# Routing tile by tile inside the mixer, with overflow work moved onto GpSimd, in a two-layer hybrid decoder trunk

## The chip, the cores and the metric

One core of one Trainium2 chip runs the whole program in one launch. The metric is device time in microseconds (us). The engines are TensorE (PE, with its weight loads as PEld), VectorE (DVE), ScalarE (ACT), GpSimd (POOL) and SyncE (SP), which mostly issues DMAs.

## The reference, cut to what matters

There are 1024 tokens of width 1024 and two layers. Layer 0 mixes tokens with an mLSTM and a gated linear attention side by side, layer 1 with sliding-window attention. Behind each mixer stands a mixture of experts: 4 groups of 8 experts, of which a token takes the best group and in it the best two experts.

```python
def hierarchical_moe(u, wg, bg, we, be, w_gate, w_up, w_down):
...
    g_probs = jax.nn.softmax((xt @ wg).astype(F32) + bg.astype(F32), axis=-1)
    g_p, g_idx = lax.top_k(g_probs, 1)
    e_logits = ((xt @ we).astype(F32) + be.astype(F32)).reshape(t, N_GROUPS, EXPERTS_PER_GROUP)
    e_in_group = jnp.take_along_axis(e_logits, g_idx[:, :, None], axis=1)[:, 0]
    top_l, top_i = lax.top_k(e_in_group, TOP_K)
    gates = g_p * jax.nn.softmax(top_l, axis=-1)
...
    padded = (counts + MOE_BLOCK - 1) // MOE_BLOCK * MOE_BLOCK
...
        return (jax.nn.silu(xb @ w_gate[e]) * (xb @ w_up[e])) @ w_down[e]
...
    out = jnp.zeros((t, d), F32).at[tok_buf].add(y_buf.astype(F32) * w_buf[:, None])
...
    for layer in range(DEPTH):
        j = layer // 2
        u = rmsnorm(h, mix_norm[layer])
...
        h = h + mix.astype(h.dtype)
        u = rmsnorm(h, ffn_norm[layer])
        h = h + hierarchical_moe(u, router_group_w[layer], router_group_b[layer], router_expert_w[layer],
...
    return rmsnorm(h, final_norm)
```

## The kernel before

The residual rows h stay in SBUF, 8 tiles of 128 tokens. A layer is a chain of blocks, and all engines meet between two of them: `layer0` or `layer1` (mixer and router product), `route` (choice of experts and the tables of rows), `experts` (one block of up to 128 rows for each of 32 experts), `experts_over` (blocks beyond the first of an expert, at run time), and last `finish`.

**layer0** (L135 to L1225) works on eight tiles in a software pipeline over t = 0 to 10. Tile t has its scores, states and heads; tile t-2 = u has `turn_out` (L537, transposes of the mixed rows) and `project_out` (L551, the output product), tile t-3 = v has `turn_rows` (L564, transposes for the router), `route_product` (L577), `turn_logits` (L585). The order on TensorE is written out in `between` (L589): pieces of the output product fill the gaps between the pieces of the newest tile. On GpSimd `gate_outputs` (L340, L343) multiplies the mixed rows by their gates, which lie in four slots that are loaded again. On VectorE the residual is added in halves (`residual`, L1164), `router_rows` (L1170, L1177) makes the normed rows, which are stored to DRAM (`u_rows`) and turned for the router; `take_logits` (L1180) adds the bias; `probabilities` (L1099) and `mask_att` (L1106) follow the scores of the newest tile. ScalarE has `h_root` (L875, squares and root), `router_cols` (L881) and `copy_logits` (L887).

**layer1** (L1866 to L2480) has the same tail: `project_out` (L2126, products on L2022), `residual` (L2413), `router_rows` (L2418), `turn_rows` (L2132), `route_product` (L2140), `turn_logits` (L2151).

**route** (L1228 to L1431) works for all eight tiles at once: some 30 VectorE instructions choose two experts a token, four wide matmuls rank the tokens of each expert (L1280 to L1283), some 40 VectorE instructions find places and columns, 32 matmuls make the tables of rows (L1287), four instructions finish them (L1425 to L1431). SP loads the first six expert units (1 MB each) in this block (`first_units`, L1852, L1858).

**experts** (L1439 to L1730). An expert has six units of 1 MB (gate, up and down, two halves each). ScalarE rounds a unit (`make_hi`, L1630), VectorE subtracts for the remainder (`make_lo`, L1691), TensorE multiplies three times (L1579). Rows come with an indirect DMA that GpSimd issues (`gather`, L1529) and go back with another (`scatter`, L1516). `turn_x` (L1563, L1566) transposes the gathered rows, `x_high` and `x_low` (L1695) split them, `silu_times_up` (L1702) and `hid_low` (L1706) stand between the products. GpSimd runs in a fixed order for expert e: scatter of e-1, gather of e+3, then `finish`, which waits until the scatter has landed. Both have this form, with two pairs of buffers:

```python
nc.gpsimd.tensor_copy(idx_y[j][:], rows_y[:, ds(e, 1)])   # L1519; gather L1530
pool.drain()                                              # L1520; gather L1531
pool.indirect_dma_start(...)                              # L1521; gather L1532
```

Of the kernel before, what the change touches and what calls it, by code (L numbers as in the profile page):

```python
# [73 lines left out]

def make_constants(nc, mem, A):

    c = {}
    for name, shape, dt in (
# [4 lines left out]
        ("by_channel", [P, 44], F32), ("channel_rows", [44, P], F32),  # L83
# [5 lines left out]
              ("conv_b", A["ab_conv_b"][0], 4)] + [(f"conv_w{j}", A["ab_conv_w"][0, j], 4) for j in range(CONV_K)]  # L89
    at, row_loads = 0, []  # L90
# [19 lines left out]
def fill_patterns(nc, c, pool):  # L110
# [20 lines left out]
    nc.gpsimd.memset(c["tri_gla"][0:GLA_CHUNK, GLA_CHUNK:P], 0.0)  # L131
    pool.drain()


def layer0(nc, c, A, h, row_loads, const_loads, logits, router, gate_rows, u_rows):  # L135
# [5 lines left out]
    T, SLOTS, RAW, UNITS = 8, 4, 3, 9  # L141
    with ExitStack() as ctx:
        mem = Memory(nc, ctx, "l0")
        with ExitStack() as under:
            u_hi, u_lo = split_tensor(Memory(nc, under, "l0u"), "u", [P, T, 8, P])
# [12 lines left out]
        slots = mem.sb("slots", [P, SLOTS, 1024])  # L158
        s_odd = [mem.sb(f"s_odd{j}", [P, 2, DV]) for j in range(2)]
# [5 lines left out]
        with ExitStack() as under:  # L165
            first = Memory(nc, under, "l0s")
            small_raw = first.sb("small_raw", [P, 8, 40])
            small_hi, small_lo = split_tensor(first, "small", [P, 8, 40])
        shifted = mem.sb("shifted", [P, T, 4, P])
        arena = mem.sb("arena", [P, 4 * (CONV_K - 1 + 1024) + 4096])  # L170
# [19 lines left out]
        root, scale, logit_cols, square = mem.sb("root", [P, T]), mem.sb("scale", [P, T]), mem.sb("logit_cols", [36, P]), mem.sb("square", [P, DV])  # L190
# [5 lines left out]
        P_, Q_ = bank(2), bank(3)  # L196
        inter_of = lambda t: pairs[1 if t == 0 else 0][:, 0:720].rearrange("p (h n) -> p h n", h=4)
# [11 lines left out]
                 "logits_copied", "logits_turned", "logits_made")  # L209
# [14 lines left out]
        with nc.Block() as block:  # L224

            @block.sync
            def _(sp):
# [28 lines left out]
                sp.dma_start(router[:, :, 0:4], A["router_group_w"][0].rearrange("(p k) n -> p k n", p=P)).then_inc(s["router_ready"], 16)  # L256
                sp.dma_start(router[:, :, 4:36], A["router_expert_w"][0].rearrange("(p k) n -> p k n", p=P)).then_inc(s["router_ready"], 16)
# [23 lines left out]
                load_gates(3)  # L281
                load_x_again(0)
                load_x_again(1)
                for t in range(T):
# [4 lines left out]
                    if t + SLOTS < T:  # L289
                        sp.wait_ge(stored[t % SLOTS], 16 * (t // SLOTS + 1))  # L290
                        sp.wait_ge(s["r_turned"], 2 * t + 2)
                        load_gates(t + SLOTS)
                for j in range(SLOTS):
                    sp.wait_ge(stored[j], 16 * 2)
# [3 lines left out]
            def _(pool):  # L298
# [41 lines left out]
                def gate_outputs(t):  # L340
                    pool.wait_ge(s["rows_scaled"], t + 1)
                    pool.wait_ge(gates_ready[t % SLOTS], 16 * (t // SLOTS + 1))
                    g.tensor_tensor(h[:, t], h[:, t], slots[:, t % SLOTS], ALU.mult).then_inc(s["rows_gated"], 1)  # L343

# [3 lines left out]
                for t in range(T):  # L348
                    gate_outputs(t)
                    if t + 3 < T:  # L350
                        end_keys(t + 3)

            @block.tensor
            def _(pe):
# [182 lines left out]
                def turn_out(u, half):  # L537
                    if half == 0:
# [4 lines left out]
                        if u >= 2:  # L543
                            pe.wait_ge(s["logits_made"], u - 1)
# [19 lines left out]
                def turn_rows(u, half):  # L564
                    if half == 0:
                        pe.wait_ge(s["r_rows_made"], u + 1)
                        if u + 1 < T:
                            pe.wait_ge(s["o_lo_made"], 2 * u + 4)
                        else:
                            pe.wait_ge(s["logits_made"], u)  # L570
                    else:
                        pe.wait_ge(s["r_cols_made"], 2 * u + 1)
                    for k in range(4 * half, 4 * half + 4):
                        last = nc.tensor.transpose(Q_[:, (k % 4) * P:(k % 4 + 1) * P], slots[:, u % SLOTS, k * P:(k + 1) * P], c["ident"][:])
                    last.then_inc(s["r_turned"], 1)

                def route_product(u):  # L577
                    pe.wait_ge(s["r_cols_made"], 2 * u + 2)
                    if u == 0:
                        pe.wait_ge(s["router_ready"], 32)  # L580
                    for k in range(8):
                        last = mm(Q_[0:36, 0:P], router[:, k], r_cols[:, k], start=(k == 0), stop=(k == 7))
                    last.then_inc(s["r_done"], 1)

                def turn_logits(u):  # L585
                    pe.wait_ge(s["logits_copied"], u + 1)
                    nc.tensor.transpose(Q_[:, 0:36], logit_cols[:], c["ident"][0:36, 0:36]).then_inc(s["logits_turned"], 1)

                def between(t, part):  # L589
# [6 lines left out]
                    elif part == 0:  # L596
                        if late:
                            project_out(u - 1, 1, 5, 7)
                    elif part == 1:
# [7 lines left out]
                    elif part == 3:  # L607
                        if here:
                            project_out(u, 0, 0, 4)
                    elif part == 4:  # L610
                        if here:
                            project_out(u, 0, 4, 8)
                        if late:
                            turn_rows(u - 1, 0)
                    elif part == 5:
                        if here:
                            project_out(u, 1, 0, 2)
                        if late:
                            turn_rows(u - 1, 1)
                    elif part == 6:  # L620
                        if here:
                            project_out(u, 1, 2, 4)
                        if late:
                            route_product(u - 1)
# [604 lines left out]

# [204 lines left out]

# [1132 lines left out]
```

## Time and profile before

| | us |
|---|---|
| median of 3 runs (lowest, highest) | 2441.41 (2437.42, 2445.01) |
| profiled execution, its own time | 2433.56 |
| its span | 2431.8 |
| PE, DVE, ACT, POOL busy | 2121.2, 1553.9, 1335.4, 419.3 |
| mean granted TensorE clock | 0.929 of full speed |

In the span the stages lie so: layer0 0 to 585, route 586.5 to 622.2, experts 622.9 to about 1248, layer1 1254 to 1716.6, route 1717.7 to 1753, experts 1753.9 to about 2383, finish to the end. No overflow block runs: in `experts_over` GpSimd clears one tile and the block ends. A timeline line gives the start, the length, the engine, the line, output and input, and in brackets the idle time of the engine just before and what ended it.

### The profile page before, as it was taken

How to read it: one execution, taken by the hardware profiler on the slowest of the kernel's cores; microseconds unless marked ns; L12 is line 12 of the kernel's file. 1: busy time of each engine (PE TensorE's matmuls, PEld its weight loads, DVE VectorE, ACT ScalarE, POOL GpSimd, SP SyncE). 2: the span in 40 equal slices, each digit the busy share in tenths (PEclk: the TensorE clock that was granted, in tenths of full speed). 3: DMA queues.
4: the chain of work that ended last, by engine and by line, in shares of the span. 5: the costliest groups of instructions: out<-in, count | busy, mean ns of one | idle time of the engine just before them, and what ended most of it. 6: DMA issues, size and time to landing. Idle time of an engine off the chain costs nothing. (4 is left out here: it accounts for less than half of the span.)

```text
span 2431.8 us, 29766 instructions
## 1 busy us (share of the span) xinstructions
PE 2121.2 (87%) x10467; PEld 1735.8 (71%) x10467; DVE 1553.9 (64%) x1591; ACT 1335.4 (55%) x1648; POOL 419.3 (17%) x381
## 2 busy tenths in 40 slices
PE   6989998985699999999959988899389999999990
PEld 5768876774588777877747867778378777777780
DVE  3551234443688888887845367623488888888885
ACT  4322334541488777777743256622078777777772
POOL 1200001110123222222213400000012222222220
PEclk9989998997799999999979978999699999999995
DMA  3112212113499999999943020000289999999975
GB/s 120 35 44 78 77 53 105 53 61 121 175 371 382 371 361 348 360 362 343 369 177 111 1 78 1 1 27 35 116 313 374 356 354 357 369 360 352 359 280 224
DMA packets 122120, 512.90 MB, mean 211 GB/s; under 512 B 27133, under 2 KB 28218, under 8 KB 87226
## 3 DMA queue, kind: packets, MB, share of 16 engines
q1 hardware_dynamic: 102458, 474.08, 52.7%
q0 software_dynamic: 18432, 33.60, 3.7%
q10 hardware_dynamic: 1152, 4.19, 0.5%
q8 instruction: 47, 0.77, 0.1%
q14 instruction: 31, 0.25, 0.0%
HBM read 495.02 MB, written 50.33 MB: 224 GB/s over the span
## 5 line engine op out<-in xcount | busy, mean ns | idle before, releaser
L1691 DVE TENSOR_TENSOR exp_w_lo<-ring_raw,exp_w_hi 128x2048 fp32r<-128x2048 f32 x384 | 866.4, 2289 | 105.5 <-ACT exp_w_hi L1630 104.9
L1630 ACT ACTIVATE exp_w_hi<-ring_raw 128x2048 fp32r<-128x2048 f32 x384 | 729.0, 1917 | 154.9 <-PE exp_y_out L1579 78.0
L1579 PE MATMUL exp_gate_out<-exp_w_hi,exp_x_hi 128*128 128x512 f32 x512 | 208.2, 407 | 11.8 <-DVE exp_w_lo L1691 10.7
L1579 PE MATMUL exp_y_out<-exp_w_hi,exp_hid_hi 128*128 128x512 f32 x512 | 211.7, 413 | 3.8 <-DVE exp_hid_lo L1706 3.8
L1579 PE MATMUL exp_y_out<-exp_w_lo,exp_hid_hi 128*128 128x512 f32 x512 | 205.4, 401 | 0.0
L1579 PE MATMUL exp_y_out<-exp_w_hi,exp_hid_lo 128*128 128x512 f32 x512 | 204.7, 400 | 0.0
L1579 PE MATMUL exp_gate_out<-exp_w_hi,exp_x_lo 128*128 128x512 f32 x512 | 201.9, 394 | 0.0
L1579 PE MATMUL exp_gate_out<-exp_w_lo,exp_x_hi 128*128 128x512 f32 x512 | 201.7, 394 | 0.0
L1579 PE MATMUL exp_up_out<-exp_w_hi,exp_x_lo 128*128 128x512 f32 x512 | 199.3, 389 | 0.0
L1579 PE MATMUL exp_up_out<-exp_w_hi,exp_x_hi 128*128 128x512 f32 x512 | 199.2, 389 | 0.0
L1579 PE MATMUL exp_up_out<-exp_w_lo,exp_x_hi 128*128 128x512 f32 x512 | 199.2, 389 | 0.0
L1521 POOL DMA_INDIRECT y_rows<-exp_y,exp_idx_y x64 | 114.1, 1783 | 374.1 <-issue 374.1
L1532 POOL DMA_INDIRECT exp_x_rows<-u_rows,exp_idx_u x64 | 101.3, 1583 | 423.4 <-DMA y_rows<-exp_y,exp_idx_y 370.0
L2022 PE MATMUL l_wide<-l_w_hi,l1s_work 128*128 128x512 f32 x512 | 170.6, 407 | 4.0 <-DVE l_w_lo L2349 3.5
L1695 DVE TENSOR_TENSOR exp_x_lo<-exp_x_turned,exp_x_hi 128x1024 fp32r<-128x1024 f32 x64 | 78.3, 1224 | 104.1 <-ACT exp_x_hi L1634 104.1
L1566 PE MATMUL exp_x_turned<-base_ident,exp_x_rows 128*128 128x128 f32 x512 | 75.5, 296 | 62.2 <-DMA exp_x_rows<-u_rows,exp_idx_u 61.9
L1634 ACT ACTIVATE exp_x_hi<-exp_x_turned 128x1024 fp32r<-128x1024 f32 x64 | 64.7, 1011 | 116.6 <-PE exp_x_turned L1566 116.6
L1579 PEld LDWEIGHTS exp_gate_out<-exp_w_hi,exp_x_hi 128*128 128x128 f32 x512 | 97.5, 190 | 31.6 <-issue 13.0
L1566 PEld LDWEIGHTS exp_x_turned<-base_ident,exp_x_rows 128*128 128x128 f32 x512 | 63.9, 151 | 76.6 <-DMA exp_x_rows<-u_rows,exp_idx_u 71.5
L1579 PEld LDWEIGHTS exp_y_out<-exp_w_hi,exp_hid_hi 128*128 128x128 f32 x512 | 100.9, 197 | 23.6 <-DVE exp_hid_lo L1706 4.3
L2022 PEld LDWEIGHTS l_wide<-l_w_hi,l1s_work 128*128 128x128 f32 x512 | 97.9, 191 | 27.6 <-DVE l_w_lo L2349 3.7
L1579 PEld LDWEIGHTS exp_y_out<-exp_w_hi,exp_hid_lo 128*128 128x128 f32 x512 | 99.6, 194 | 21.8
(418 smaller groups left out, 4016.1 us busy)
## 6 DMA issues: line engine op xcount, KB each, us to landing
ring_raw<-in_expert_w_gate_dram SPq DMA_DIRECT2D x128, 1024.0 KB
ring_raw<-in_expert_w_up_dram SPq DMA_DIRECT2D x128, 1024.0 KB, 11.7
ring_raw<-in_expert_w_down_dram SPq DMA_DIRECT2D x128, 1024.0 KB, 8.3
l0w_raw<-in_ab_w_in_dram SPq DMA_DIRECT2D x48, 256.0 KB, 2.8
l_q<-y_rows SPq DMA_DIRECT2D x8, 1024.0 KB, 5.1
finish_y<-y_rows SPq DMA_DIRECT2D x8, 1024.0 KB
base_h<-in_x_dram ACTq DMA_DIRECT2D x8, 512.0 KB, 6.9
gate_rows<-l0w_stage SPq DMA_DIRECT2D x16, 256.0 KB, 2.0
```

The costliest lines, as they stand in the source:

```text
L1521: pool.indirect_dma_start(y_rows, bass.IndirectOffsetOnAxis(ap=idx_y[j][:], axis=0), y[j][:], None, bounds_check=2047, oob_is_err=False).t ...
L1532: pool.indirect_dma_start(x_rows[j][:], None, u_rows, bass.IndirectOffsetOnAxis(ap=idx_u[j][:], axis=0), bounds_check=1023, oob_is_err=Fal ...
L1566: last = nc.tensor.transpose(x_turned[:, k], x_rows[j][:, k * P:(k + 1) * P], c["ident"][:])
L1579: last = nc.tensor.matmul(out, x[:, k0 + k], w[:, k, cols], start=(first and k == 0 and t == 0), stop=(last_unit and k == K - 1 and t == 2))
L1630: nc.scalar.activation(split[split_slot(unit)][0][:], raw[raw_slot(unit)][:], ACT.Copy).then_inc(hi_ready, 1)
L1634: nc.scalar.activation(x_hi[:], x_turned[:], ACT.Copy).then_inc(x_hi_s, 1)
L1691: nc.vector.tensor_tensor(lo[:], raw[raw_slot(unit)][:], hi[:].bitcast(F32), ALU.subtract).then_inc(lo_ready[split_slot(unit)], 1)
L1695: nc.vector.tensor_tensor(x_lo[:], x_turned[:], x_hi[:].bitcast(F32), ALU.subtract).then_inc(x_cols_s, 1)
L2022: last = nc.tensor.matmul(out_cols[:, cols], x[:, k], w[:, k, cols], start=(k == 0 and n == 0), stop=(k == 7 and n == 2))
```

## The change

1. `route` is gone. After a tile's logits VectorE chooses its experts (`choose_experts`, 16 instructions of a [128, 4] or [128, 32] size, most with a drain behind), TensorE ranks its tokens (`rank`, two matmuls) and enters them in the table (`enter`, two matmuls), one and two tiles late, in part 5 of `between`. The last tile's share and `make_tables` end layer0 and layer1.
2. The router reads rows of h that are not normed: the ffn gains are multiplied into the router on GpSimd once, the transposes take h itself, the scale is put in with the bias. The product has the rows stationary and the 36 router columns moving, so `copy_logits` and `turn_logits` go. `router_rows` becomes `scale_of` and `normed_rows`; the latter is called later in VectorE's order and only the store waits for it.
3. The gates' multiplication goes from GpSimd to VectorE (`gate_rows_of`), with three slots for four; the clearing of the two gather tiles too.
4. What is needed for overflow blocks alone (number of blocks, first columns, columns of tokens, one-hot marks, owners) is 76 GpSimd instructions in six pieces among the first six scatter and gather pairs of `experts`. Sixteen matmuls and a second `make_tables` for it end `experts`.
5. The first six expert units are loaded in layer0 and layer1; `experts` begins with `make_hi` of two units, and the weights of the two choices are worked out in it.
6. In layer 1 output product, residual and row transposes go by halves, and the order by tiles is changed with them.

```diff
-                gather(0, 0)
-                gather(1, 1)
-                for e in (2, 3):
-                    pool.wait_ge(x_turned_s, e - 1)
-                    gather(e, e % 2)
...
+                for e in range(4):
+                    if e < 2:
+                        pool.wait_ge(zeroed, e + 1)
+                    else:
+                        pool.wait_ge(x_turned_s, e - 1)
+                    gather(e, e % 2)
+                def scatter_and_gather(pair, q):
+                    e = 2 * pair + 1 + q
+                    scatter(e - 1, q)
+                    pool.wait_ge(x_turned_s, e + 2)
+                    gather(e + 3, q)
+                    finish(q, pair)
+                scatter_and_gather(0, 0)
+                count_blocks()
+                scatter_and_gather(0, 1)
+                first_columns()
+                scatter_and_gather(1, 0)
+                columns_of_tokens()
+                scatter_and_gather(1, 1)
+                mark_rest(0, 8)
+                scatter_and_gather(2, 0)
+                mark_rest(8, N)
+                scatter_and_gather(2, 1)
+                owners()
+                with pool.Fori(3, last_pair - 1) as pair:
...
+                def first_columns():
+                    g.tensor_copy(extra[:], above[:, 0:E, 0])
+                    g.tensor_copy(nth[:], above[:, E:, 0])
+                    pool.drain()
...
+                    for step in (1, 2, 4, 8, 16):
+                        g.tensor_copy(b[:, 0:step], a[:, 0:step])
+                        g.tensor_tensor(b[:, step:], a[:, step:], a[:, 0:E - step], ALU.add)
+                        pool.drain()
+                        a, b = b, a
...
+                def mark_rest(first_n, end_n):
+                    for n in range(first_n, end_n):
+                        g.tensor_scalar(slot_hot[:, n], c["iota"][:], slot[:, n:n + 1], None, ALU.is_equal)
+                        last = g.tensor_scalar(block_hot[:, n], c["iota"][:, 0:N_OVER], column[:, n:n + 1], value[:, n:n + 1], ALU.is_equal, ALU.mult)
...
+def choose_experts(v, dve, c, R, logits, t):
...
+    v.tensor_tensor(R.masked, R.masked, logits[:, t, 4:36], ALU.add)
+    for k in range(2):
+        dve.drain()
+        v.tensor_reduce(R.top[:, k, t:t + 1], R.masked, AX.X, ALU.max)
+        dve.drain()
+        v.scalar_tensor_tensor(R.flags, R.masked, R.top[:, k, t:t + 1], far, ALU.is_ge, ALU.mult)
...
                     elif part == 5:
                         if here:
                             project_out(u, 1, 0, 2)
                         if late:
-                            turn_rows(u - 1, 1)
+                            route_product(u - 1)
+                        if 1 <= u - 1 < T - 1:
+                            rank(u - 2, ranks)
+                        if 2 <= u - 1 < T - 1:
+                            enter(u - 3, entered)
+                        if t == T + 2:
+                            enter(T - 2, last_entered)
+                            rank(T - 1, last_ranks)
+                            enter(T - 1, last_entered)
+                            count()
```

## Rows read from the trace of the kernel before

**Rows 1.** The page: busy time by engine; ScalarE's costliest group, with its mean in ns.
```profile
PE 2121.2 (87%) x10467; PEld 1735.8 (71%) x10467; DVE 1553.9 (64%) x1591; ACT 1335.4 (55%) x1648; POOL 419.3 (17%) x381
...
L1630 ACT ACTIVATE exp_w_hi<-ring_raw 128x2048 fp32r<-128x2048 f32 x384 | 729.0, 1917 | 154.9 <-PE exp_y_out L1579 78.0
```

**Rows 2.** Busy time by stretch: window, length, PE, PEld, DVE, ACT, POOL, clock, DMA share, GB/s.
```profile
400.00:450.00 50.00, 49.62 (x334) 39.27 (x333) 23.23 (x53) 23.96 (x73) 6.17 (x6) 1.00 0.19 64
572.17:637.88 65.71, 17.97 (x74) 15.09 (x74) 29.18 (x95) 9.92 (x13) 6.14 (x8) 0.53 0.29 112
1702.28:1768.80 66.52, 21.92 (x117) 18.98 (x116) 30.21 (x98) 11.18 (x17) 6.03 (x8) 0.60 0.28 110
```

**Rows 3.** Timeline of PE between the mixers' last output products and the experts' first products.
```profile
571.77 0.39 PE L560 MATMUL l_pair<-l_w_hi,l_o_lo 128*128 128x512 f32 x1
580.41 3.63 PE L582 MATMUL l_pair<-l_r_cols,base_router 128*36 128x128 f32 x16 [0.69 <-ACT l_r_cols L885]
...
637.88 0.77 PE L1579 MATMUL exp_gate_out<-exp_w_hi,exp_x_hi 128*128 128x512 f32 x1 [5.33 <-DVE exp_w_lo L1691]
...
1702.04 0.39 PE L2022 MATMUL l_wide<-l_w_hi,l1s_work 128*128 128x512 f32 x1
```

**Rows 4.** Timeline of POOL at the start of both expert stages, and of DVE in route.
```profile
622.91 1.84 POOL L1512 MEMSET exp_x_rows<- 128x1024 f32 x2 [84.87 <-POOLq L57]
...
1753.93 1.84 POOL L1512 MEMSET exp_x_rows<- 128x1024 f32 x2 [341.22 <-POOLq L57]
...
590.25 0.22 DVE L1299 SCALAR_TENSOR_TENSOR route_flags<-base_iota,route_flags 128x64 f32<-128x64 f32 x1
590.55 0.22 DVE L1301 TENSOR_REDUCE route_idx<-route_flags 128x8 f32<-128x64 f32 x1
```

**Rows 5.** Timeline of layer 0's mixer: DVE, then POOL's gate product.
```profile
426.59 0.69 DVE L1104 SCALAR_TENSOR_TENSOR l_prob<-l_pair,l_shifted 128x512 f32<-128x512 f32 x1 [7.03 <-PE l_pair L466]
...
437.67 2.14 DVE L1177 SCALAR_TENSOR_TENSOR l_slots<-base_h,l_scale,l_gain_row 128x1024 f32<-128x1024 f32 x1
...
535.69 2.35 POOL L343 TENSOR_TENSOR base_h<-base_h,l_slots 128x1024 f32<-128x1024 f32 x1 [21.99 <-ACT base_h L866]
```

**Rows 6.** Layer 0's first expert stage: busy times, and what its PE waited for.
```profile
640.00:1230.00 590.00, 567.14 (x2624) 468.20 (x2624) 498.07 (x282) 444.98 (x313) 148.62 (x118) 0.98 0.95 357
PE exp_x_turned L1566 <- DMA exp_x_rows<-u_rows,exp_idx_u: 20.7, 10, 3.3
```

**Rows 7.** Lines L1531 and L1532: duration min/median/max in ns; time to landing.
```profile
L1531 POOLq DRAIN  x64: 242/9109/10644, 624.9 to 2325.9; - x64
DMA to landing us min/median/max: 4.1/8.6/10.7
```

**Rows 8.** Timeline of POOL in the first experts of layer 0.
```profile
677.16 1.68 POOL L1530 COPY exp_idx_u<-moe_rows_u 128x1 int32 x1
684.48 2.34 POOL L1532 DMA_INDIRECT exp_x_rows<-u_rows,exp_idx_u  x1 [5.63 <-DMA y_rows<-exp_y,exp_idx_y]
...
734.88 1.95 POOL L1530 COPY exp_idx_u<-moe_rows_u 128x1 int32 x1
742.47 2.23 POOL L1532 DMA_INDIRECT exp_x_rows<-u_rows,exp_idx_u  x1 [5.64 <-DMA y_rows<-exp_y,exp_idx_y]
...
764.61 0.20 POOL L1519 COPY exp_idx_y<-moe_rows_y 128x1 int32 x1
773.00 2.33 POOL L1521 DMA_INDIRECT y_rows<-exp_y,exp_idx_y  x1 [8.19 <-issue]
```

**Rows 9.** Timeline in the same stretch: PE's transposes of gathered rows, DVE's subtractions.
```profile
701.88 1.03 PE L1566 MATMUL exp_x_turned<-base_ident,exp_x_rows 128*128 128x128 f32 x8
...
734.49 4.53 DVE L1691 TENSOR_TENSOR exp_w_lo<-ring_raw,exp_w_hi 128x2048 fp32r<-128x2048 f32 x2 [0.52 <-ACT exp_w_hi L1630]
```

**Rows 10.** Groups of POOL instructions, shapes apart: count, busy us, mean ns, idle before.
```profile
L1519 POOL COPY exp_idx_y<-moe_rows_y 128x1 int32 x56 | 48.9, 873 | 57.1 <-ACT exp_y L1650 57.1
L1530 POOL COPY exp_idx_u<-moe_rows_u 128x1 int32 x56 | 41.1, 734 | 0.0
```

More of the change, by code:

```diff
@@ new lines, in rank_tokens, with take_ranks, mark_places @@
+def rank_tokens(mm, c, R, logits, t, ranks):
+    mm(ranks, c["tri_strict"][:], R.both[:, t], start=True, stop=False)
+    return mm(ranks, c["ones"][:], logits[:, t, 4:36], start=False, stop=True)
+def take_ranks(v, R, t, ranks):
+    return v.tensor_tensor(R.work, R.hot[:, :, t], bc(ranks, 1, 2), ALU.mult)
+def mark_places(v, dve, c, R, t):
+    v.tensor_reduce(R.pos[:, :, t], R.work, AX.X, ALU.add)
+    v.tensor_tensor(R.block_hot[t % 2], R.hot[:, :, t], bc(c["value"][:, :, t], 2, N_EXPERTS), ALU.mult)
+    dve.drain()
+    for k in range(2):
+        last = v.tensor_scalar(R.slot_hot[t % 2][:, k], c["iota"][:], R.pos[:, k, t:t + 1], None, ALU.is_equal)
+    return last
@@ new lines, in enter_tokens, with take_entries, make_tables @@
+def enter_tokens(mm, R, t, entered):
+    for k in range(2):
+        last = mm(entered, R.slot_hot[t % 2][:, k], R.block_hot[t % 2][:, k], start=(k == 0), stop=(k == 1))
+    return last
+def take_entries(v, R, t, entered):
+    if t == 0:
+        return v.tensor_copy(R.made[:], entered)
+    return v.tensor_tensor(R.made[:], R.made[:], entered, ALU.add)
+def make_tables(v, dve, made, rows_y, rows_u, none, table):
+    v.tensor_scalar(none, made, 0.0, float(UNUSED + 1), ALU.is_equal, ALU.mult)
+    dve.drain()
+    v.scalar_tensor_tensor(table, made, -1.0, none, ALU.add, ALU.add)
+    dve.drain()
+    v.tensor_copy(rows_y[:], table)
+    dve.drain()
+    return v.tensor_scalar(rows_u[:], rows_y[:], 1, None, ALU.logical_shift_right)
@@ new lines, in load_first_units, with moe @@
+def load_first_units(sp, A, layer, raw, raw_ready):
+    for m, (name, e) in enumerate((("expert_w_gate", 0), ("expert_w_up", 0), ("expert_w_gate", 1))):
+        src = A[name][layer, e].rearrange("(p a k) n -> a p k n", p=P, a=2)
+        for half in range(2):
+            s = 2 * m + half
+            sp.dma_start(raw[s][:].rearrange("p (k n) -> p k n", k=4), src[half]).then_inc(raw_ready[s], 16)
+def moe(nc, c, A, layer, R, logits, weight, u_rows, y_rows, raw, raw_ready):
+    with ExitStack() as ctx:
+        Memory(nc, ctx, f"ring{layer}").sb("raw", [P, len(raw), 2048])
+        experts(nc, c, A, layer, R, logits, weight, u_rows, y_rows, raw, raw_ready)
+    experts_over(nc, c, A, layer, R, u_rows, y_rows)
@@ L89, in make_constants @@
               ("conv_b", A["ab_conv_b"][0], 4)] + [(f"conv_w{j}", A["ab_conv_w"][0, j], 4) for j in range(CONV_K)]
+    params += [(f"ffn_gain{layer}", A["ffn_norm"][layer], 8) for layer in range(2)]
     at, row_loads = 0, []
@@ L609, in between @@
                             project_out(u, 0, 0, 4)
+                        if late:
+                            turn_rows(u - 1, 1)
                     elif part == 4:
@@ L1866, in layer1 @@
-def layer1(nc, c, A, h, weight, y_rows, logits, router, u_rows):
+                    if 0 <= w < T - 1:
+                        normed_rows(w)
+                take_late_entries(T - 2)
+                place_late(T - 1)
+                take_late_entries(T - 1)
+                make_tables(v, dve, R.made[:], R.rows_y, R.rows_u, R.masked, R.flags)
+                dve.wait_ge(s["counted"], 1)
+                v.tensor_copy(R.counts[:], counted)
+def layer1(nc, c, A, h, weight, y_rows, logits, router, u_rows, R, raw_ring, ring_ready):
```

1383 lines of the change are left out of this document (715 added, 668 removed).

## The prediction

> **What bounds the kernel now.** I read the page first. PE is busy 87% of the span, POOL 17% [rows 1]; that average hides three regimes, so I asked for busy times by stretch. In the steady mixer of layer 0 PE is busy 49.62 of 50 us: work added to PE there is added time. Between the last output product of a mixer and the first expert product PE has 18.0 of 65.7 us and 21.9 of 66.5 us of work [rows 2]; that is where the change can win. In the expert stage of layer 0 PE is busy 567 of 590 us, and all but 2 us of the rest is its wait for gathered rows, ten times, 20.7 us in all [rows 6]. So GpSimd, nearly idle in the page, runs a chain whose pace is that of PE or a little worse: index copy, drain, indirect DMA, twice an expert. The reader should see what the chain is made of: the copy is a column of 128 numbers, but the drain behind it has a median of 9.1 us, against 0.24 us when nothing is in flight, about a landing (8.6 us) [rows 7]. In the timeline the gather at 684.48 stands 5.6 us behind the copy begun at 677.16, and the scatter at 773.00 stands 8.2 us behind its copy [rows 8]. What is added to this chain behind a landing moves the next gather one for one, and PE with it once the lead is used up. The lead: gather of expert 4 is issued at 684.48, lands 8.6 later at 693, and is needed at 701.88 [rows 8, 9], so 8 to 9 us; expert 7's is issued at 742.47, landed by 751, and needed three PE periods of 17.71 after 701.88, at 755.0: 4 us are left.
>
> **What is saved, layer 0.** The last product ends at 572.16 and the expert stage begins at 622.91 [rows 3, 4]: 50.7 us. What takes its place: 3.4 us from that end to the router product (8.2 now, at 580.41 [rows 3]; the normed rows, 2.1 us [rows 5], leave the path, and so do the transposes and copies of the first half, done earlier; between 3 and 5); the product at the cold clock 3.6 [rows 3], 16 matmuls as now; the logits 0.5; `choose_experts`, 16 dependent instructions at the 0.30 us between two such in route [rows 4], 4.8; six matmuls of rank and enter at 0.23 each (3.63 by 16 [rows 3]), 1.4, with some eight VectorE steps between and behind them, 2.4, and their hops, 1.1; the change of block 1.5. Sum 18.7, so **32 us** saved. Layer 1 has 1702.43 to 1753.93, 51.5 us [rows 3, 4]; there VectorE comes to the last residual with an older tile's logits and normed row (2.1) still ahead, so 21: **30 us** saved.
>
> **Start of the experts.** From 622.91 to the first product at 637.88 are 15.0 us [rows 3, 4]. The first weights' rounding (1.9 [rows 1]) and remainder (2.3, from 4.53 for two [rows 9]) now run while the gather is under way, and clearing on VectorE lets the gather start 1.2 earlier: less 5.4, plus the remainder of the gathered rows, half a weight's size, 1.2, which now ends last. So 10.8, **4.2 us** saved, twice. The six loads' own landing (11 to 12 us) is no longer behind anything. Early loads fall where the mixer's DMA share is 0.19 [rows 2]: hidden; cover gone would cost their landing. Saved in all: 32 + 30 + 8.4 = **71 us**.
>
> **What the mixers pay.** PE in layer 0 gets four small matmuls more and one transpose less a tile, 0.6 us net, eight times 5, uncovered since PE is full [rows 2]. VectorE gets choosing (4.8), the gates' product (2.35 on POOL [rows 5]; half a weight's subtraction in size, so 1.2 here) and marks, and loses nothing but the place of the normed row. It has 23 of 50 us now [rows 2], so there is room, but order matters: `probabilities` stands in its queue behind the new steps, and PE's next transposes wait for it. Today VectorE has been idle 7.0 us before it [rows 5]; the new chain after the product takes some 8, so 1.2 us late in four tiles, 5. The last two tiles, where PE has nothing else, wait for later outputs and marks, 8. Layer 1 pays 0.7 a tile, 5.6. Two more row loads at the start 0.7, matmuls and tables at the end of each expert stage 2 each. Sum **28 us**; from 15, if VectorE is always early, to 50. Moving the gates off GpSimd saves nothing by itself: its product had waited 22 us for its input [rows 5].
>
> **What GpSimd pays: 76 instructions a layer in the chain above.** Before shows no such instruction in this stage but the two copies, so I bound the price. Low: 0.20 us for a copy that met nothing [rows 8] and 0.24 for a free drain [rows 7]: 0.44. High: at 734.88 a copy took 1.95 us; VectorE's subtraction had begun at 734.49, 2.27 each, and the copy ended at 736.83, with the first of the two [rows 8, 9]. All 56 looped copies of either kind have means of 0.87 and 0.73 [rows 10], four times the free 0.20, in a stage where VectorE is busy 498 of 590 [rows 6]. I take that mean, 0.80, and a drain: 1.04. Of the 76, 32 are marks, without drains, issued while a scatter or gather lands: 16 × 0.80 = 12.8 less 8.2 of the drain that would have waited anyway [rows 8] is 4.6, twice, 9. The other 44 have drains; the first drain takes up the landing, so the rest is exposed: 46. Together 55; less the lead, 8: 47. Something comes back: when PE stands, ring loads stop and landings shorten, at most from 8.6 to the least of 4.1 [rows 7], two an expert in six experts, 54; but only part of the time, and I take 16. So 31 us a layer, **62 us**, all on the path.
>
> The copies' behaviour has a rule in the Trainium skill, page SBUF — State Buffer, section "SBUF: two separate sides": the port pair that GpSimd shares with VectorE is an exclusive lock for a whole instruction, held also by a VectorE instruction with two SBUF inputs against a GpSimd one that reads SBUF. By that rule, the trace agrees (1.95 against 0.20), all 76 instructions are exposed to it, not the copies alone, and it speaks against the change. Without it 76 cheap instructions would be the low price.
>
> **Forecast.** 71 saved, 28 and 62 paid: 19 us slower. The profiled execution would have 2433.6 + 19 = 2453; it lies 8 under the median of the runs, so on their footing 2441.4 + 19 = **2460**. Its own range is 2440 to 2485.
>
> **Rivals.**
> A. *The pieces run clear of VectorE.* If most small instructions fall in VectorE's gaps, or the lock doesn't touch them, each costs 0.44: 44 × 0.44 = 19, marks hidden, less the lead 8, less 5 of shorter landings: 6 a layer. Then 71 - 28 - 12 = 31 faster, **2410** (2398 to 2430). For it: the copy at 764.61 took 0.20 [rows 8]. Against: the means of rows 10.
> B. *Strict turns (slower).* Each GpSimd instruction waits for one whole VectorE instruction. 282 of them stand in 590 us with 92 us of gaps [rows 6], so a PE period of 17.7 has 8.5, and 2.8 us of gaps for six more: 14.5 of ours in 17.7, 1.22 each. 44 × 1.22 + 2 × (19.5 - 8.2) = 76, less 8 and 16: 52 a layer, **2502**. It decides from about 0.85 us an instruction on, drain included: above that the 43 us won before this stage are gone.
> C. *The new VectorE chain stalls layer 0's mixer (slower).* If `probabilities` or the output product waits for the whole 4.8 us of choosing, not 1.2, in each of six tiles: 22 us more, **2482**. For it: PE has no slack there [rows 2]; against: VectorE is busy less than half.
> D. That the change doesn't do what it says (loads held by their waits, so that the first product comes as now) costs 4 to 8 us and lies within the ranges.
>
> **Chances.** Forecast 0.43, A 0.30, B 0.14, C 0.13. The range that leaves out no more than 2 in 10 is 2402 to 2500. A measurement of this kernel can tell 0.3%, 7.3 us, from no change. Faster by more than that: all of A and a little of the forecast's low end, 0.31; within it, that end between 2434 and 2449, 0.10; slower 0.59.
>
> **What would show it.** In the profile after: first expert product about 45 us nearer to the end of each mixer than 65.7 and 66.4 now, of that 11 us after the stage's start; PE's waits for gathered rows near 20.7 + 31 us in layer 0 [rows 6], nearly all new ones between experts 4 and 11, at the pieces; small GpSimd instructions with a mean of 0.8 us, long ones ending with a VectorE subtraction; steady mixer tiles grown by 1 to 2. A is right if those instructions have a mean of 0.3 and the new waits are under 10 us; B if the mean is over 1.0; C if the mixer of layer 0 is over 30 us longer. The prediction is wrong in kind if PE waits for weights in place of rows, or if landings shorten so much that the chain gains its lead back within six experts.

## The result

The changed kernel has a median of 2481.65 us (4 runs, 2474.62 to 2483.84) against 2441.05 for the kernel before on the same chip: a ratio of 1.0161, 95% interval 1.0134 to 1.0188. It is slower by 41 us where 19 were forecast. The profiled executions lie further apart, 2483.36 (span 2481.3) against 2433.56: 50 us, which is what the traces must account for.

Laid over the spans of the two, the 49.4 us fall like this (first or last matmul of each stage; the difference is after minus before, rounded):

| stretch | before | after | difference |
|---|---|---|---|
| layer 0, start to the first output product | 380.7 | 387.0 | +6.3 |
| to the last output product's end | 191.4 | 210.8 | +19.4 |
| to the first expert product | 65.7 | 29.6 | -36.1 |
| to the last down product | 605.8 | 648.8 | +43.0 |
| to layer 1's first matmul | 23.3 | 22.8 | -0.5 |
| layer 1's mixer, to the last product's end | 435.5 | 442.6 | +7.1 |
| to the first expert product | 66.4 | 33.6 | -32.7 |
| to the last down product | 609.0 | 652.3 | +43.3 |
| to the end | 54.1 | 53.8 | -0.2 |

Busy time by stretch of the changed kernel (window, length, PE, PEld, DVE, ACT, POOL, clock, DMA share, GB/s), to be held against [rows 2, 6]:

```profile
443.40:471.90 28.50, 25.99 (x178) 20.92 (x178) 16.76 (x50) 13.26 (x44) 1.22 (x2) 1.00 0.17 56
597.80:627.38 29.58, 10.54 (x46) 9.34 (x45) 17.87 (x47) 9.59 (x11) 3.86 (x5) 0.50 0.27 90
1741.54:1775.17 33.63, 11.88 (x52) 11.07 (x52) 21.30 (x58) 9.58 (x11) 3.95 (x5) 0.54 0.23 81
628.00:1276.00 648.00, 589.45 (x2681) 485.89 (x2680) 507.20 (x290) 449.30 (x316) 210.35 (x197) 0.95 0.87 324
```

Both gaps are half of what they were. The expert stage of layer 0 has some 59 us in which PE is not busy, where it had 23 [rows 6], and PE's list of waits says for what:

```profile
PE exp_x_turned L412 <- DMA exp_x_rows<-u_rows,exp_idx_u: 54.2, 12, 12.6
```

The same line had 20.7 us, ten times, longest 3.3. These waits grew by 33.5 us and the stage by 43.0. The other 9 are PE's own busy time, at a lower granted clock; the same busy times from the first expert product to the last down product, before and after:

```profile
637.88:1243.70 605.82, 581.07 (x2680) 479.18 (x2680) 505.47 (x286) 450.53 (x317) 150.52 (x121) 0.98 0.93 349
627.38:1276.16 648.78, 590.23 (x2683) 486.57 (x2683) 507.31 (x290) 449.92 (x317) 210.35 (x197) 0.95 0.87 324
```

So the list of waits shows less than what GpSimd holds up. The timeline of POOL shows the second and the fourth of the six pieces, with a piece of VectorE's timeline behind them:

```profile
708.33 2.33 POOL L361 DMA_INDIRECT exp_x_rows<-u_rows,exp_idx_u  x1 [7.08 <-DMA y_rows<-exp_y,exp_idx_y]
710.66 1.40 POOL L287 COPY exp_extra<-exp_above 128x32 f32<-128x32 f32 x1
712.01 0.19 POOL L288 COPY exp_nth<-exp_above 128x16 f32<-128x16 f32 x1
717.54 0.28 POOL L290 TENSOR_SCALAR exp_slot<-exp_nth 128x16 f32<-128x16 f32 x1 [5.34 <-issue]
...
722.46 2.39 POOL L350 DMA_INDIRECT y_rows<-exp_y,exp_idx_y  x1 [0.85 <-issue]
...
753.84 1.38 POOL L361 DMA_INDIRECT exp_x_rows<-u_rows,exp_idx_u  x1 [3.74 <-issue]
755.26 1.70 POOL L323 TENSOR_SCALAR exp_slot_hot<-base_iota,exp_slot 128x128 f32<-128x128 f32 x1
756.97 4.64 POOL L324 TENSOR_SCALAR exp_block_hot<-base_iota,exp_column,base_value 128x16 f32<-128x16 f32 x1
761.60 0.59 POOL L323 TENSOR_SCALAR exp_slot_hot<-base_iota,exp_slot 128x128 f32<-128x128 f32 x1
762.18 0.42 POOL L324 TENSOR_SCALAR exp_block_hot<-base_iota,exp_column,base_value 128x16 f32<-128x16 f32 x1
...
777.35 2.22 POOL L350 DMA_INDIRECT y_rows<-exp_y,exp_idx_y  x1 [0.94 <-issue]
...
756.90 4.56 DVE L546 TENSOR_TENSOR exp_w_lo<-ring_raw,exp_w_hi 128x2048 fp32r<-128x2048 f32 x2 [0.42 <-ACT exp_w_hi L480]
761.39 0.68 DVE L557 TENSOR_TENSOR exp_hid<-exp_silu,exp_up_out 128x512 f32<-128x512 f32 x1
```

A gather and the next scatter stand 14.1 and 23.5 us apart here, 8.5 to 10.5 before. The instruction on 16 columns that ran from 756.97 to 761.61 began while VectorE had started two subtractions, 756.90 to 761.46, and ended 0.15 behind them. Two lines on, the same instruction takes 0.42.

In layer 0's mixer a new wait stands at 372 us, on VectorE, and behind it one on PE:

```profile
372.00 1.23 DVE L1848 TENSOR_TENSOR base_h<-base_h,l_slots 128x1024 f32<-128x1024 f32 x1 [11.97 <-DMA l_slots<-gate_rows]
...
373.55 0.69 DVE L1779 SCALAR_TENSOR_TENSOR l_prob<-l_pair,l_shifted 128x512 f32<-128x512 f32 x1
...
374.29 1.11 PE L1148 MATMUL l_pair<-base_ident,l_prob 128*128 128x128 f32 x4 [5.89 <-DVE l_prob L1779]
```

### The profile page after: what moved, and what is told of

Its sections match the earlier page's. It is cut to its first block and busy times, and to the rows that moved or that the text cites. A ratio compares the mean times of both kernels' runs of the same rounds, so it can differ in the third digit from the quotient of the medians.

```text
span 2481.3 us, 30458 instructions
## 1 busy us (share of the span) xinstructions
PE 2139.1 (86%) x10571; PEld 1756.3 (71%) x10571; DVE 1598.3 (64%) x1821; ACT 1331.3 (54%) x1632; POOL 519.5 (21%) x530
## 5 line engine op out<-in xcount | busy, mean ns | idle before, releaser
L425 PE MATMUL exp_y_out<-exp_w_hi,exp_hid_hi 128*128 128x512 f32 x512 | 217.5, 425 | 3.8 <-DVE exp_hid_lo L561 3.8
L412 PE MATMUL exp_x_turned<-base_ident,exp_x_rows 128*128 128x128 f32 x512 | 81.2, 310 | 127.6 <-DMA exp_x_rows<-u_rows,exp_idx_u 127.6
L359 POOL COPY exp_idx_u<-base_rows_u 128x1 int32 (+1 forms) x64 | 48.3, 755 | 500.1 <-DVE exp_x_rows L565 484.3
L425 PEld LDWEIGHTS exp_y_out<-exp_w_hi,exp_hid_lo 128*128 128x128 f32 x512 | 102.4, 200 | 23.3
L425 PEld LDWEIGHTS exp_y_out<-exp_w_lo,exp_hid_hi 128*128 128x128 f32 x512 | 103.3, 202 | 20.2
```

Of the source, the lines that this page charges most:

```text
L359: nc.gpsimd.tensor_copy(idx_u[j][:], rows_u[:, ds(e, 1)])
L412: last = nc.tensor.transpose(x_turned[:, k], x_rows[j][:, k * P:(k + 1) * P], c["ident"][:])
L425: last = nc.tensor.matmul(out, x[:, k0 + k], w[:, k, cols], start=(first and k == 0 and t == 0), stop=(last_unit and k == K - 1 and t == 2))
```

## The experiments

Theory P: the pieces stand in GpSimd's chain, and what they add behind a landing moves all later gathers. Its rivals say that the stages grew for another reason, or that it is the number of drains, or that instructions are slow by themselves. All ratios are to the kernel before, with 95% intervals.

**1. Without the overflow work.**

```diff
-                count_blocks()
...
-                owners()
-                pe.wait_ge(over_placed, 1)
...
-                make_tables(v, dve, made[:], R.over_y, R.over_u, none[:], table[:])
+                v.memset(R.over[:], 0)
```

> The changed kernel with its 76 overflow instructions a layer left out, and the sixteen matmuls and the second tables with them; the number of overflow blocks is set to zero, which is what it is here. Theory P (the pieces stand in GpSimd's chain of scatters and gathers, and push every later gather): each expert stage falls from 649 to 652 us back to 606 to 612, so the kernel from 2481.7 to about 2400; the interval between gather 4 and gather 11 in layer 0 falls from 174 us to about 134. Rival S (the stage grew because of the earlier start, the new order at its start or the clock): the stages stay above 630 us and the kernel above 2440.

Measured: 2410.45 us, ratio 0.9885 (0.9866 to 0.9905). The expert stages took 609.8 and 608.9 us; gather 4 to gather 11 in layer 0 took 138.8 us, 174.1 with the pieces, 134.1 in the kernel before. P holds for the stages, though the kernel is 10 us above the 2400 expected. Without the pieces the rest of the change wins 30 us.

**2. The pieces behind the last scatter.**

```diff
                 scatter(E - 1, 1)
+                count_blocks()
+                first_columns()
+                columns_of_tokens()
+                mark_rest(0, 8)
+                mark_rest(8, N)
+                owners()
                 finish(0, last_pair)
```

> The changed kernel with the same six pieces moved behind the last scatter of the expert block, where VectorE and the rings are idle. Theory P: the stages up to the last down product are as without the pieces, 606 to 612 us, and the pieces cost their own time at the end, some 20 to 25 us a layer, so about 2445. If the contention with VectorE is what makes the single instructions long, the mark instructions take their 0.42 and 0.59 us here every time and the first subtraction well under 2.3 us; if such instructions are slow by themselves (rival), the means stay 0.9 to 1.0 us for marks and 2.4 for the first subtractions, and the kernel is at about 2470.

Measured: 2486.22 us, ratio 1.0196 (1.0176 to 1.0216). The stages to the last down product are 607.7 and 606.9 us, as P says, and the instructions are short. The groups of the marks, first here, then in the changed kernel (count, busy us, mean ns):

```profile
L323 POOL TENSOR_SCALAR exp_slot_hot<-base_iota,exp_slot 128x128 f32<-128x128 f32 x32 | 19.2, 601 | 0.3 <-issue 0.3
L324 POOL TENSOR_SCALAR exp_block_hot<-base_iota,exp_column,base_value 128x16 f32<-128x16 f32 x32 | 13.7, 428 | 0.0
```

```profile
L324 POOL TENSOR_SCALAR exp_block_hot<-base_iota,exp_column,base_value 128x16 f32<-128x16 f32 x32 | 32.8, 1026 | 0.0
L323 POOL TENSOR_SCALAR exp_slot_hot<-base_iota,exp_slot 128x128 f32<-128x128 f32 x32 | 27.5, 859 | 0.2
```

All 152 together take 66.2 us here, a mean of 0.44, and 124.2 there, a mean of 0.82. But laid end to end with their drains they last from 1241.05 to 1279.58, 38 us a layer and not the 20 to 25 that I had written: my price for a free instruction came from a copy of one column, and the marks take 0.42 to 0.60 and the wide ones up to 1.5.

**3. The pieces ahead of the first scatter.**

```diff
+                count_blocks()
...
+                owners()
                 scatter_and_gather(0, 0)
-                count_blocks()
                 scatter_and_gather(0, 1)
```

> The changed kernel with all six pieces ahead of the first scatter, where GpSimd has been idle for 20.3 us. The pieces took 62 us of instructions a layer beside VectorE (mean 0.82) and 33 us alone. Theory P (every us that GpSimd spends beyond its idle time moves the whole chain, and the 8 us by which gather 4 comes early are no lead, since the chain at 19.1 us an expert uses them up by itself): about 9 us of landing, then some 45 to 50 us of instructions and drains, less 20 idle: the stages grow by 30 to 38 us over 608, the kernel is at 2470 to 2480. Rival (the lead is real and absorbs 8 more): 2455 to 2462. Rival (the six separate drains behind a landing are the cost, and one block has only one): the stages grow by under 15 us, about 2435.

Measured: 2478.14 us, ratio 1.0149 (1.0093 to 1.0204), stages of 648.1 and 635.2 us, 40 and 27 over 608. One block with one landing costs about as much as six, in layer 0 at least: from 645.64 to 717.2, 72 us, of which some 20 had been idle. Gather 4 came 44.5 us later against the first transposes than in the kernel before; of that 41 us were left at the last gather's transposes in layer 0, 23 of 43 in layer 1, where 27 gathers took 500 us and not the 513 of layer 0. What gave those 20 us back was not found, so that the chain carries on every delay in full is shown for layer 0 and for run 4, and not for every case. The rival on the drains falls: one block, with one landing behind it, is far from under 15 us.

**4. A delay in the kernel before.**

```diff
+                both(0, 0)
+                pool.drain()
+                for n in range(11):
+                    nc.gpsimd.memset(waste[:], 0.0)
+                    pool.drain()
+                both(0, 1)
```

> The kernel before, with one delay a layer on GpSimd: behind the gather of expert 4 a drain and eleven clearings of an unused tile of 1024 columns (0.95 us each by the row of such a clearing, with drains some 12 us). It tests the step that took 8 us of lead off what GpSimd pays. Theory N (no lead: the chain of 19.1 us an expert uses up those 8 us by expert 8 with or without the delay, and whatever stands in the chain comes out at its end): each expert stage grows by 10 to 13 us, and the kernel by 20 to 26, to about 2464. Rival (the lead absorbs 8 us): each stage grows by 2 to 5 us, the kernel by 4 to 10, to about 2448. Second rival (later landings shorten and give it back): under 4 us in all.

Measured: 2461.64 us, ratio 1.0093 (1.0067 to 1.0119), 23 us. The stages grew by 13.8 and 12.0 us, from 605.8 and 609.0 to 619.6 and 621.0. The timeline shows the delay that was put in:

```profile
687.02 1.04 POOL L1533 DMA_INDIRECT exp_x_rows<-u_rows,exp_idx_u  x1 [7.74 <-DMA y_rows<-exp_y,exp_idx_y]
694.86 11.72 POOL L1553 MEMSET exp_waste<- 128x1024 f32 x11 [6.79 <-issue]
```

From the gather of expert 4 to the next scatter the two layers took 12.3 and 14.4 us longer, and 13.8 and 12.0 came out at the stages' ends, some 570 us later. The lead of 8 us absorbed nothing.

**5. Scatters and gathers written out, in the kernel before.**

```diff
-                    nc.gpsimd.tensor_copy(idx_y[j][:], rows_y[:, ds(e, 1)])
-                    pool.drain()
-                    pool.indirect_dma_start(y_rows, bass.IndirectOffsetOnAxis(ap=idx_y[j][:], axis=0), y[j][:], None,
+                    pool.indirect_dma_start(y_rows, bass.IndirectOffsetOnAxis(ap=rows_y[:, e:e + 1], axis=0), y[j][:], None,
...
-                with pool.Fori(0, last_pair - 1) as pair:
+                for pair in range(last_pair - 1):
```

> The kernel before with the scatters and gathers of all 32 experts written out, so that each indirect DMA takes its column of the row table directly and the index copy and the drain behind it are gone. Theory D (the drain, which lasts until the DMA in flight has landed, makes scatter and gather take turns, 19.1 us a pair against PE's 17.7): the expert stages fall from 606 and 609 us to about 578, PE's waits for gathered rows vanish behind the first experts, and the kernel is at about 2385. Rival Q (the indirect DMA waits for its turn by itself, in its queue or its descriptor writing): the interval between gathers stays 19 us and the kernel within 10 us of 2441.

Measured: 2374.50 us, ratio 0.9731 (0.9715 to 0.9747), 66 us faster than the kernel before. The stages took 575.1 and 574.9 us. Timeline of POOL, busy times of the stage, and PE's waits for rows in the whole span, of which the two are the stages' first gathers:

```profile
726.09 1.21 POOL L1519 DMA_INDIRECT y_rows<-exp_y,moe_rows_y  x1 [15.17 <-ACT exp_y L1646]
727.61 1.02 POOL L1528 DMA_INDIRECT exp_x_rows<-u_rows,moe_rows_u  x1 [0.31 <-issue]
743.87 1.13 POOL L1519 DMA_INDIRECT y_rows<-exp_y,moe_rows_y  x1 [15.24 <-ACT exp_y L1646]
745.31 1.02 POOL L1528 DMA_INDIRECT exp_x_rows<-u_rows,moe_rows_u  x1 [0.31 <-issue]
...
636.00:1211.00 575.00, 571.04 (x2680) 473.80 (x2680) 503.52 (x286) 449.66 (x317) 83.03 (x60) 0.99 0.96 367
...
PE exp_x_turned L1562 <- DMA exp_x_rows<-u_rows,moe_rows_u: 18.1, 2, 9.3
```

Scatter and gather are now issued 1.5 us apart; the drain between them had kept GpSimd for 5.6 us [rows 8], and another stood ahead of each scatter. A pair takes 17.7 us, PE's pace, and GpSimd idles for 15 of them. So theory D holds: what the run took away, copy, drain and loop together, had cost 66 us. That it was the drains is read from the trace of the kernel before and not from a run of its own: in each layer, from the gather of expert 4 on, the 28 drains ahead of a scatter and the 28 ahead of a gather all ended 0.07 or 0.08 us behind the landing of the indirect DMA issued before them, while the copies had means of 0.87 and 0.73 us [rows 10].

**6. The same on the changed kernel, pieces in place.**

> The changed kernel with scatters and gathers written out as in the run on the kernel before (no index copy, no drain), pieces where the change has them. Theory D: a gather then comes 25.5 us ahead of its transposes, 16 more than it needs, and GpSimd idles 14 of 17.7 us, so the pieces disappear: both stages at about 577 us in place of 649 and 652, the kernel at 2335 to 2345. Rival (the drains inside the pieces wait for landings as before and a piece of 20 us is longer than the slack): the stages stay at 590 to 600 and the kernel at 2365 to 2385.

Measured: 2395.43 us, ratio 0.9818 (0.9767 to 0.9868). The stages took 601.5 and 597.7 us: the rival's size. The kernel is 10 us above what the rival said. The stages grew by 25 and 21 us over the 576.5 and 576.3 that they take without pieces (run 7), where they had grown by 39 and 43: the slack hid somewhat less than half. With a piece between them a gather and the next scatter stand up to 30 us apart, 16.2 without.

**7. The pieces dealt out, three instructions to an expert.** With the copies and drains of the change first:

```diff
+                for pair in range(last_pair - 1):
+                    for q in range(2):
+                        scatter_and_gather(pair, q)
+                        play(3)
```

> The changed kernel with its index copies and drains, and the same 76 instructions dealt out three to an expert. Theory P (in a chain without idle time it is the time behind a landing that counts, however it is cut): the 44 instructions with drains cost 0.8 to 1.0 us each as before, the 32 marks vanish behind landings, now all of them; the stages grow by 30 to 45 us over 608, against 41 and 43, the kernel at 2465 to 2485. Rival (small portions hide in a landing): under 15 us of growth, the kernel under 2435.

Measured: 2443.50 us, ratio 1.0012 (0.9988 to 1.0036), stages of 625.7 and 630.6 us. Neither expectation: the growth over 608 is 18 and 23, half of that of six pieces, though the instructions themselves took 227 us in all, a mean of 1.49. The trace says where: in layer 0 the 27 intervals from a gather to the next scatter sum to 308.7 us, 55 more than before, so what GpSimd adds there is as much as theory P says and as with six pieces (302.3). But those from a scatter to the next gather sum to 228.2, 35 less than before, where six pieces left 6 less: the scatters landed in 7.6 us on the mean and not in 8.9. Why small portions shorten the scatters' landings is open. Then with scatters and gathers written out and the gates' product on GpSimd:

> The changed kernel with scatters and gathers written out (no index copy, no drain), the gates' multiplication on GpSimd, and the 76 overflow instructions dealt out three to an expert over 26 experts in place of six pieces. Theory P (what counts is how much GpSimd adds between a gather and the next scatter, against its 14 us of idle time an expert): three instructions of 0.8 us behind one landing of 8 us fit, both stages at 575 to 578 us where six pieces left 601 and 598, the kernel at 2340 to 2350. Rival (each drain in GpSimd's order costs a landing wherever it stands, and now there are drains behind every gather): the stages stay near 600 and the kernel at 2390.

Measured: 2340.63 us, ratio 0.9604 (0.9555 to 0.9654): 100 us under the kernel before and 141 under the changed one, and the fastest here. It is 34 us under run 5, so of the 100 us about 66 are the chain's and 34 the change's own. The stages took 576.5 and 576.4 us, PE was busy 571.69 of 576:

```profile
622.00:1198.00 576.00, 571.69 (x2680) 474.62 (x2681) 505.45 (x290) 448.75 (x317) 178.59 (x136) 0.99 0.96 364
...
PE exp_x_turned L433 <- DMA exp_x_rows<-u_rows,base_rows_u: 17.7, 2, 9.3
```

Without the overflow work:

> As the first kernel of this call with the overflow work left out. Theory P: it differs from the first by the 36 to 60 us of GpSimd instructions a layer being hidden, so by no more than 5 us in all; the kernel at 2338 to 2345. Rival: if the dealt-out instructions still cost, this one is 20 or more us faster than the first.

Measured: 2349.97 us, ratio 0.9645 (0.9595 to 0.9695). It isn't faster, so the dealt-out work is hidden whole. It is 9 us slower all the same; its expert stages are equal (576.5, 576.3), and the 9 us lie behind the last down products, 4.5 ahead of layer 1's first matmul and 5 ahead of the end. There the trace shows GpSimd's drain that closes the expert block, first in this run, then with the work dealt out:

```profile
L233 POOLq DRAIN  x2: 5284/5285/5286, 1205.6 to 2294.6; - x2
L233 POOLq DRAIN  x2: 707/707/707, 1203.5 to 2292.4; - x2
```

It begins when the last scatter has landed and still takes 5.3 us, 4.6 more than with the work dealt out, once a layer. Its length goes with the indirect DMAs that GpSimd issued since its last drain: 0.12 us behind one (the kernel before), 0.71 behind 8, 3.97 behind 48 (run 6), 5.3 to 5.4 behind 64 (here and in run 5), about 0.08 us for each. So the dealt-out work, hidden itself, saves this with its drains, and run 5 loses some 5 us a layer in the same place.

**8. The mixer of layer 0.** Gates on GpSimd again, then the choosing behind the probabilities:

```diff
-                    if 1 <= t <= T:
-                        gate_rows_of(t - 1)
```

> The changed kernel with the gates' multiplication on GpSimd again, all else as changed, three slots too. Theory G (VectorE, waiting for the gate rows' load, holds up the probabilities behind it): the first output product of layer 0 comes at 382 in place of 388, the steady tiles lose about 1 us each of their 28.6, and the kernel is 8 to 12 us faster, about 2471. Rival L (the gate rows are simply late with three slots and the product would wait for them on any engine): the first output product stays at 387 to 388 and the kernel within 3 us of 2481.

Measured: 2479.27 us, ratio 1.0161 (1.0144 to 1.0178). The first output product came at 380.1, 6.9 us earlier, as theory G says. But only 3.6 of them were left at the last one (594.2 against 597.8), and the kernel is not the 8 to 12 us faster that was expected. In layer 1, which this edit doesn't touch, the mixer took 456.6 us against 442.6 and the expert stage 637.0 against 652.3, so that the two nearly cancel. The stage's 15 us are not explained. The mixer ran at a lower granted clock (0.89 against 0.97 in the like stretch of 100 us):

```profile
1500.00:1600.00 100.00, 84.50 (x608) 72.86 (x604) 72.29 (x144) 58.03 (x174) 0.00 (x0) 0.89 0.00 1
```

```profile
1504.00:1604.00 100.00, 81.58 (x644) 71.00 (x643) 76.04 (x154) 63.32 (x189) 0.00 (x0) 0.97 0.00 1
```

```diff
-                        take_logits(w)
                     if t + 1 < T:
                         probabilities(t + 1)
                         mask_att(t + 1)
+                    if 0 <= w < T:
+                        choose(w)
```

> The changed kernel with the 16 choosing instructions and the marks of layer 0 called behind the probabilities of the newest tile; only the three that read the router's bank stay ahead. Theory C (in the mixer of layer 0 PE waits 1.4 to 1.6 us a tile for probabilities that stand behind the choosing): those waits vanish, tiles of 28.6 become about 27, the last output product comes 4 to 7 us earlier than 597.8, the kernel is at about 2476. Rival: the wait for the low part of the turned rows (0.9 us a tile) grows instead and the kernel stays at 2481.

Measured: 2501.26 us, ratio 1.0246 (1.0194 to 1.0298), 20 us above the changed kernel and outside both expectations. Tiles of 28.6 us became 34.6. PE's wait for probabilities is gone and its wait for the low part of the turned rows grew from 15.8 to 35.1 us:

```profile
446.50:481.10 34.60, 28.62 (x178) 23.29 (x177) 16.81 (x50) 13.19 (x43) 1.22 (x2) 0.89 0.13 47
...
PE l_pair L1214 <- DVE l_o_lo L1837: 35.1, 7, 7.4
```

With both edits and the written-out chain:

> The same with the gates' multiplication on GpSimd and the choosing of layer 0 behind the probabilities, all edits that helped. If they add up: 4 to 10 us under the run without these two, about 2333. If the mixer's gains are lost again at its end, where the last two tiles wait for VectorE: within 3 us of it.

Measured: 2419.78 us, ratio 0.9921 (0.9896 to 0.9946), 24 us above the run without the two (run 6). The last output product of layer 0 came at 616.3, 18 us later than there: the choosing's new place cost more than the gates gave. Another 8 us lie in layer 1's mixer, which neither edit touches.

## Why the forecast had the sign and not the size

By its own steps, in the profiled execution, where it said 19 and 49 came. Of the 30 us missed 24 lie in the expert stages and 8 in layer 0's mixer; the rest nearly cancels.

*Gaps between mixer and experts.* 71 forecast (its parts sum to 70.4), 68.9 measured (36.1 and 32.7). Of the parts, in layer 0: the router's product was in place 3.2 us after the last output product and took 3.63; the expert stage's first transposes came at 623.04 and its first product 4.34 later, 7.30 before. Right.

*Layer 0's mixer.* 18 forecast, 25.6 measured. The tiles from the first output product on grew by 19.4. The steady ones grew by 2.6 to 2.8, where 1 to 2 was the sign: PE waits up to 1.6 for probabilities and 0.9 for the turned rows, 0.2 before. The first two hardly grew, and the last two by 8.3 together, where 8 was said. So the step is right, and its sum in part by luck. The other 6.3 are a wait that the prediction passed over when it said that moving the gates saves nothing by itself. The gates' product waits for its rows from DRAM; on GpSimd nothing needed stood behind that wait; on VectorE the keys, the probabilities and PE do. Run 8 shows it: with the product back on GpSimd these 6.3 us are gone.

*Layer 1's mixer.* 5.6 forecast, 7.1 measured, and that they agree is luck. In the eleven kernels here that have the changed mixer of layer 1 it took 442.6 to 456.7 us, at mean granted clocks from 0.94 down to 0.90, and 442.6 is the shortest. The mixer of before took 434.8 to 440.2 us in three kernels, 435.5 at 0.92 in the profile of before. At 0.92 the changed one took 448.6 to 448.8: some 13 us more, and not 5.6.

*Ends of the expert stages.* 4 us forecast for matmuls and tables behind them, nothing measured (-0.5 and -0.2).

*The expert stages.* 62 forecast for the pieces, 86 more in the two stages. The price of an instruction came out right, 0.80 said and 0.82 measured over all 152, but by two errors that cancel: alone they take 0.44 (run 2) and not 0.20, and VectorE adds 0.38 and not 0.60. What was exposed was a little less than said: the six intervals from a gather to the next scatter sum to 104.4 us in layer 0, and to 58.3 before, 46.1 more where 55 were forecast. Two terms behind it failed. **"Less the lead, 8"** should have been nothing: the chain takes 19.1 us an expert (27 gathers in 516 us) and PE 17.7, so it uses the 8 us up by expert 8, with the pieces or without, and a delay ahead of that is carried on. Run 4 shows it alone. And **"something comes back ... I take 16"** was 8.5: the intervals from a scatter to the next gather sum to 60.1 against 68.6, two of the seven shortened to 6.2 and 4.1, the others hardly. 46.1 - 8.5 and 2.4 more in the next interval are the 40 that gather 11 is late, where the prediction had 31. The last 3 us of the 43 are of the size of the earlier first product: the chain begins with the first gathers and not with it, so of the 4.2 us saved at the stage's start only about 1 could reach the end. Other terms of up to 3 us, later in the chain and at its two ends, cancel. The sign "waits near 20.7 + 31" came true with 54.2, but again by luck: the stage grew by more than its waits, since PE's own work took 9 us longer.

*Rivals.* A falls by the mean of 0.82. B, 2502, is a little nearer to 2482 than the forecast, but not in kind: strict turns would give 1.22 an instruction. Most ran free (the median of the small mark is 0.418), and of its 32 three waited for two subtractions. PE stopped, VectorE stopped with it, and the pieces then ran at full speed: contention eases itself here. The means bear this out: 0.44 with VectorE idle, 0.82 here, 1.05 and 1.15 where PE stood less (runs 6 and 7, written out), 1.49 in portions with drains. C's time, 2482, is the measured one, by luck: it wanted layer 0's mixer over 30 us longer, which was 25.6, with 2.7 us a tile and not 5, and the rest lies in the expert stages. Run 8 shows how near the bigger loss is.

The Trainium skill's rule (page SBUF — State Buffer, section "SBUF: two separate sides", an exclusive lock for the whole instruction) agrees in kind with the trace: 0.42 us alone, and 4.64 for the one that ended 0.15 behind a subtraction. That it waited for a second subtraction too is more than the rule says. What it alone would have led to is B, and the mean of 0.82 stays well under that.

## What to carry to other kernels

Before work is put on an idle engine, ask whether that engine issues a chain whose pace is the bound, and time the chain (here 19.1 us against 17.7) and not the engine's busy share (17%). A lead that a slower chain uses up by itself is no cover. Where a drain stands between two DMAs, try to remove what needs it first: here 66 us lay there (with the copies and the loop), and once they were gone the same overflow work, in portions smaller than the new slack, cost nothing. And a step that waits for a DMA is not moved to an engine in whose queue the bound engine's inputs stand.

## What was not expected of the hardware

A GpSimd drain behind an indirect DMA lasts until that DMA has landed: it ended 0.07 or 0.08 us behind the landing, and the drains have medians of 8.2 and 9.1 us in the kernel before. Without it two indirect DMAs were issued 1.5 us apart, and both still landed in time, though a gather then took 11.2 us to land in place of 8.6. The drain put off to the end of the block cost some 0.08 us for each indirect DMA issued since the last one, 5.3 us for 64. An indirect DMA took its indices straight from a column of a wide table. The same mixer of layer 1, with the same order, took from 442.6 to 456.7 us in eleven kernels of this study, at mean granted clocks from 0.94 down to 0.90; differences of under 14 us in time between kernels that differ elsewhere have to be looked for by stage.
